# First attention of a two-block transformer: the sum of a modulation row moved behind a head pair's projection products

## The chip, the cores and the metric

The kernel runs on one core of a Trainium2 chip. The time is device microseconds of one execution, from start to end. Three runs of the kernel before took 1410.66, 1416.59 and 1410.87 us; the median is 1410.87 us. One execution was profiled.

## The reference, cut to what matters

The reference is two transformer blocks over 256 tokens of width 1024, batch 1, in float32. The first block is modulated: a vector `c` goes through a matrix `w_ada` of 1024 x 6144, and the six pieces of the result shift, scale and gate the two halves of the block. Its mixer has two attentions of eight heads each; the first is ordinary softmax attention here (there is one block of 256 keys), with a bias by distance.

```python
c_act = jax.nn.silu(c)
mod = c_act @ w_ada[l] + b_ada[l]
sh_m, sc_m, gt_m, sh_f, sc_f, gt_f = jnp.split(mod, 6, axis=-1)
h = modulate(rms_norm(x, g_mix[l]), sh_m, sc_m)
proj = jnp.einsum('bsd,de->bse', h, w_in[l])
qa, ka, va, qb, kb, vb, gate_logits = jnp.split(proj, splits, axis=-1)
oa = moba_attention(...)            # first attention: qa, ka, va
ob = stick_breaking_attention(...)  # second attention: qb, kb, vb
...
x = x + gt_m[:, None, :] * mixed
```

## The kernel before, in words

Every large product is done in three parts: a float32 matrix is split into a high part and a remainder, and high times high, high times remainder and remainder times high are added up in PSUM (L2808 to L2812). A unit is 4 x 128 rows by 512 columns of a weight matrix. SyncE's queue loads it into one of three `raw` buffers, ScalarE writes its high part (`split_hi`, L2077), VectorE its remainder (`split_lo`, L2339), and TensorE then runs 24 matmuls on it: 4 row tiles, 2 tiles of 128 tokens, 3 parts. In the stretch in question three split buffers go round, and a step that works on unit u first orders the splitting of unit u + 2 (`split_ahead`, L249).

The order of the work is written out by hand. `build_plan` adds steps to one list, and each engine goes through that list and issues its own share of each step. A step that stands earlier in the list stands earlier in every engine's queue; an engine works through its queue in order, and stands still at an instruction whose semaphores have not come.

The first attention is `softmax_heads` (L446 to L497). It works on pairs of heads. For a pair it issues the products of queries and keys (`qk`), which VectorE turns into logits (L2581); then a filler; then the transposes of the probabilities of the pair before (`probturn`, L2979, three 128x128 transposes for each head, read out by ScalarE at L2207); then the exponentials of the new pair (ScalarE, L2202); then another filler; and then the products of the older pair with its values (`pv`). The transposes of even heads go to PSUM bank 2, those of odd heads to bank 3. Before it writes a bank, TensorE waits until the bank's last tenant has been read (`wait_free`, L1788).

The fillers (the list `fa`, L1224) put other work between the attention's steps: the projection of `qb`, `kb` and `vb`, each in two units of 24 matmuls into banks 6 and 7, whose results ScalarE copies out (L2179); and the modulation rows 4 to 9, which are needed only later. For such a row VectorE multiplies `w_ada` by the column `c_act` and adds up over eight tiles in `ada_acc` (L2448, L2450). A `quarter` (L1180) is half of that, four tiles; POOL loads the next half from HBM in two pieces, as soon as VectorE is through with the piece that it replaces (L1952). After two quarters `sum_next` (L1173) issues the sum over the 128 partitions (`adasum`): TensorE waits for `ada_acc`, multiplies it by a matrix of ones into bank 3 (L2890), and VectorE adds the result to `gate_rows` (L2468). For rows 4 and 5 that is one 128x512 float32 product.

The fillers in turn: `qb` first unit with the first quarter of row 4; `qb` second unit with the second quarter of row 4; and then the step of the change, with the sum of row 4, the first quarter of row 5 and the first unit of `kb`. This third filler stands between the `qk` products of heads 2 and 3 and the transposes of the probabilities of heads 0 and 1.

Of the kernel before, what the change touches and what calls it, by code (L numbers as in the profile page):

```python
# [266 lines left out]
def build_plan(W):  # L267
# [937 lines left out]
    def chunk_fillers(name, i, dst, mode):  # L1205

        made = {}

        def first():
            made["uses"], made["parts"] = w_in_chunk(i, dst, mode, (6, 7))  # L1210
            r[name] = made["uses"]
            add_proj(made["parts"][0])

        def second():
            add_proj(made["parts"][1])
        return first, second

    heads_of = {name: chunk_fillers(name, i, i * BANK, "plain") for name, i in (("qb", 3), ("kb", 4), ("vb", 5))}
# [3 lines left out]
        turns_of("kb", 4, 12, 6, ("uses", r["kb"]))  # L1222

    fa = [[sum_next, quarter, f] for name in ("qb", "kb", "vb") for f in heads_of[name]]  # L1224
    fa += [[sum_next, turn_second], [quarter], [sum_next]]

    gates = [chunk_fillers(f"gate{i}", 6 + i, (0, BANK, 3 * BANK, 4 * BANK)[i], "tanh") for i in range(4)]
# [399 lines left out]
def program(nc, consts, x, c, w_ada, b_ada, g_mix, w_in, w_br_moba, w_br_sb, w_out, rel_bias, g_ffn, w_up,  # L1627
            w_conv, b_conv, w_down, g_final, norm_g, ffn_wg, ffn_wu, ffn_wd, even_w_in, even_w_out,
            even_lambda, even_subln, odd_w_in, odd_w_out, odd_rel_bias, table, out):
    with ExitStack() as ctx:  # L1630
# [7 lines left out]
        def over(name, handle_end, words, n):  # L1638
# [118 lines left out]
                                                                               "group_hidden"))  # L1757

        plan = build_plan(dict(w_ada=w_ada[0], w_in=w_in[0], w_br_moba=w_br_moba[0], w_br_sb=w_br_sb[0], w_out=w_out[0],
                               w_up=w_up[0], w_down=w_down[0], ffn_wg=ffn_wg, ffn_wu=ffn_wu, ffn_wd=ffn_wd,  # L1760
                               even_w_in=even_w_in, even_w_out=even_w_out, odd_w_in=odd_w_in, odd_w_out=odd_w_out))
# [1363 lines left out]
```

How the kernel before makes its waits and increments, by code:

```python
        def wait_ready(eng, use):  # L1776
            if use.unit is not None:
                eng.wait_ge(unit_used, use.unit + 1)
            else:
                eng.wait_ge(psum_ready[use.bank], use.ready)
# [1 line left out]
        def wait_read(eng, use):  # L1783
            name, value = use.read_by
            eng.wait_ge(psum_read[use.bank] if name == "psum_read" else named[name], value)
# [6 lines left out]
        def wait_past(eng, free):  # L1793
            for f in free:
                if isinstance(f, int):
                    eng.wait_ge(unit_used, f + 1)
                else:
                    wait_ready(eng, f)
# [1 line left out]
        def wait_rows(eng, what):  # L1801
            if what in raw_slot:
                eng.wait_ge(weight_loaded[raw_slot[what]], landed[what])
                return raw[:, raw_slot[what], :]
            e = plan.early.index(what[1])
            eng.wait_ge(early_landed[e % FIRST], 16 * (e // FIRST + 1))
            return early_rows[e % FIRST]
# [56 lines left out]
        @block.sync  # L1865
# [3 lines left out]
            def wait_consumed(number):  # L1869
                if isinstance(plan.ada_done[number], int):
                    sp.wait_ge(ada_used, plan.ada_done[number])
                else:
                    wait_ready(sp, plan.ada_done[number])
# [4 lines left out]
                    e = plan.early.index(what[1])  # L1878
                    if e == 2:
                        sp.wait_ge(c_act_ready, 1)
                    if e >= FIRST:
# [38 lines left out]
            def link(ins):  # L1920
                pool.wait_ge(pool_step, mark(ins))
```

## Time and profile before

| | |
|---|---|
| median of 3 runs | 1410.87 us |
| the profiled execution, whole | 1412.61 us |
| its span, first to last instruction | 1410.9 us |
| TensorE busy | 1371.5 us (97%) |
| VectorE busy | 1096.4 us (78%) |
| ScalarE busy | 817.6 us (58%) |
| mean granted TensorE clock | 0.993 of full speed |
| first attention, with fillers | about 72 to 125 us of the span |
| stretch between the `qk` products of heads 2, 3 and the next filler | 83.9 to 93.7 us |

Times in the rows count from the start of the span. A row of the timeline gives start, duration, engine, source line, operation, destination and sources, and how many equal instructions are merged in it; in brackets, how long the engine stood still before it, and on whom it waited. TensorE's rows are pipelined: the start of the next row, not the end of one, tells how fast the engine gets on.

### The profile page before, as it was taken

The page shows a single profiled execution, that of the slowest core. Times are in us where ns is not written, and L with a number is a line of the kernel's source. Part 1 is how long each engine was busy: PE and PEld are TensorE (multiplying, and loading weights), DVE is VectorE, ACT ScalarE, POOL GpSimd, SP SyncE. Part 2 cuts the span into 40 slices and gives each one's busy share as a digit, 9 for nine tenths or more (in the row PEclk, how much of TensorE's full clock was granted, in tenths as well). Part 3 has the DMA queues.
Part 4 walks back from the last instruction along what each step waited for, and adds up shares of the span by engine and source line. Part 5 has one row for each costly group of instructions (what it writes and reads, how often), then busy time and mean ns, then how long its engine had stood idle before and what let it go on. Part 6 is the DMA issues. An engine that isn't in the chain of part 4 may idle for free.

```text
span 1410.9 us, 19388 instructions
## 1 busy us (share of the span) xinstructions
PE 1371.5 (97%) x6943; PEld 1138.8 (81%) x6943; DVE 1096.4 (78%) x1565; ACT 817.6 (58%) x1301; POOL 80.3 (6%) x133
## 2 busy tenths in 40 slices
PE   4999999999999999999999999999999999999998
PEld 4878877999987888888778888888888877788886
DVE  5677787799777999669986999569996556679893
ACT  4556755755546566466576566465655567566562
POOL 3011100000000000012300000000000100000000
PEclk8999999999999999999999999999999999999999
DMA  9887556487653565745255466735747373564570
GB/s 353 287 305 257 192 174 188 147 282 248 203 185 131 183 238 166 231 131 170 99 169 169 172 222 213 234 107 203 242 151 267 116 221 120 180 204 147 201 238 30
DMA packets 160702, 274.37 MB, mean 194 GB/s; under 512 B 5953, under 2 KB 87617, under 8 KB 160609
## 3 DMA queue, kind: packets, MB, share of 16 engines
q1 hardware_dynamic: 153904, 250.86, 53.0%
q0 software_dynamic: 5552, 20.20, 4.6%
q10 hardware_dynamic: 1153, 2.07, 0.4%
q8 instruction: 57, 0.93, 0.3%
q14 instruction: 36, 0.29, 0.1%
HBM read 272.05 MB, written 1.06 MB: 194 GB/s over the span
## 4 chain that ended last, share of the span: by engine, by line
PE 68%; DVE 9%; issue 3%; DMA 2%; ACT 1%; POOL 0%; DVEq 0%; POOLq 0%; ACTq 0%; SPq 0%
PE psum L2810 17%; PE psum L2812 17%; PE psum L2811 17%; DVE w_lo L2339 3%; PE psum L2853 2%; PE psum L2852 2%; PE psum L2850 2%; PE psum L3059 2%; PE psum L3058 2%; PE psum L3057 2%; DMA raw<-in_ffn_wu_dram 1%; PE psum L3083 1%; DVE scr L2331 1%; PE psum L2907 1%; DMA raw<-in_ffn_wd_dram 1%
## 5 line engine op out<-in xcount | busy, mean ns | idle before, releaser
L2339 DVE TENSOR_TENSOR w_lo<-raw,w_hi 128x1024 fp32r<-128x1024 f32 (+2 forms) x310 | 368.0, 1232 | 72.2 <-ACT w_hi L2077 71.3
L2077 ACT ACTIVATE w_hi<-raw 128x1024 fp32r<-128x1024 f32 (+2 forms) x310 | 308.1, 1047 | 89.5 <-DMA raw<-in_ffn_wu_dram 23.7
L2810 PE MATMUL psum<-w_hi,hT_hi 128*128 128x512 f32 x712 | 287.3, 404 | 6.5 <-DVE hT_lo L2504 3.7
L2812 PE MATMUL psum<-w_hi,hT_lo 128*128 128x512 f32 x712 | 278.4, 391 | 0.0
L2811 PE MATMUL psum<-w_lo,hT_hi 128*128 128x512 f32 x712 | 278.2, 391 | 0.0
L2810 PEld LDWEIGHTS psum<-w_hi,hT_hi 128*128 128x128 f32 x712 | 134.7, 189 | 39.1 <-issue 10.0
L2812 PEld LDWEIGHTS psum<-w_hi,hT_lo 128*128 128x128 f32 x712 | 134.6, 189 | 29.1
L2811 PEld LDWEIGHTS psum<-w_lo,hT_hi 128*128 128x128 f32 x712 | 135.0, 190 | 25.7 <-issue 0.5
L2810 PE MATMUL psum<-w_hi,hc_hi 128*128 128x512 f32 x272 | 106.7, 392 | 1.6 <-DVE hc_lo L2429 1.1
L2812 PE MATMUL psum<-w_hi,hc_lo 128*128 128x512 f32 x272 | 106.0, 390 | 0.0
L2811 PE MATMUL psum<-w_lo,hc_hi 128*128 128x512 f32 x272 | 105.9, 389 | 0.0
L2339 DVE TENSOR_TENSOR lo_at<-raw,hi_at 128x1024 fp32r<-128x1024 f32 x74 | 87.3, 1220 | 8.4 <-ACT hi_at L2077 8.3
L2339 DVE TENSOR_TENSOR lo_qk<-raw,hi_qk 128x1024 fp32r<-128x1024 f32 (+1 forms) x72 | 84.0, 1208 | 5.6 <-ACT hi_qk L2077 5.6
L2077 ACT ACTIVATE hi_at<-raw 128x1024 fp32r<-128x1024 f32 x74 | 74.3, 1051 | 22.9 <-PE psum L2812 6.1
L2077 ACT ACTIVATE hi_qk<-raw 128x1024 fp32r<-128x1024 f32 (+1 forms) x72 | 71.4, 1042 | 23.7 <-DMA raw<-in_ffn_wu_dram 8.1
L2017 POOL TENSOR_TENSOR stat<-stat,minus_half 128x1 f32<-128x1 f32 (+2 forms) x24 | 17.2, 717 | 1122.5 <-DVE stat L2487 1044.5
L2235 ACT ACTIVATE PR<-psum,stat 128x256 f32<-128x256 f32 x56 | 24.2, 472 | 67.6 <-PE psum L2812 66.4
L2810 PEld LDWEIGHTS psum<-w_hi,hc_hi 128*128 128x128 f32 x272 | 51.1, 188 | 13.5 <-DVE hc_lo L2729 1.6
L2812 PEld LDWEIGHTS psum<-w_hi,hc_lo 128*128 128x128 f32 x272 | 51.1, 188 | 10.7
L2811 PEld LDWEIGHTS psum<-w_lo,hc_hi 128*128 128x128 f32 x272 | 51.1, 188 | 10.0
L2107 ACT ACTIVATE hT_hi<-psum,cols 128x128 fp32r<-128x128 f32 x96 | 27.5, 369 | 51.6 <-PE psum L2907 51.6
L2268 ACT ACTIVATE hc_hi<-psum 128x512 fp32r<-128x512 f32 (+1 forms) x32 | 17.3, 539 | 67.5 <-PE psum L3083 67.5
(301 smaller groups left out, 2864.6 us busy)
## 6 DMA issues: line engine op xcount, KB each, us to landing
raw<-in_ffn_wd_dram SPq DMA_DIRECT2D x44, 1024.0 KB, 5.0
raw<-in_ffn_wg_dram SPq DMA_DIRECT2D x56, 512.0 KB, 4.3
raw<-in_ffn_wu_dram SPq DMA_DIRECT2D x56, 512.0 KB, 5.5
raw<-in_w_up_dram SPq DMA_DIRECT2D x44, 512.0 KB, 5.0
raw<-in_w_in_dram SPq DMA_DIRECT2D x19, 1024.0 KB, 7.3
raw<-in_ffn_wg_dram SPq DMA_DIRECT2D x16, 1024.0 KB, 5.2
raw<-in_ffn_wu_dram SPq DMA_DIRECT2D x16, 1024.0 KB, 5.3
ada_raw<-in_w_ada_dram POOLq DMA_DIRECT2D x24, 512.0 KB, 5.2
```

What stands on the lines that cost most here:

```text
L2077: nc.scalar.activation(hi_of(s)[:, cs], source_of(s)[:, cs], ACT.Copy).then_inc(ready, 1)
L2107: ins = nc.scalar.activation(tiles_of(hT_hi, k0 + i, 1, a["ts"])[:, 0, :], psum[:, a["use"].bank, i * w:(i + 1) * w], ACT.Copy, scale=g)
L2339: nc.vector.tensor_tensor(lo_of(u)[:, cs], source_of(u)[:, cs], hi_of(u)[:, cs].bitcast(F32), ALU.subtract)\
L2810: nc.tensor.matmul(o, a_hi, b_hi, start=start, stop=False)
L2811: nc.tensor.matmul(o, a_hi, b_lo, start=False, stop=False)
L2812: return nc.tensor.matmul(o, a_lo, b_hi, start=False, stop=stop)
L2850: nc.tensor.matmul(o, hi[:, b], hT_hi[:, kk, :], start=kk == 0 and f % 2 == 0, stop=False, skip_group_check=True)
L2852: nc.tensor.matmul(o, hi[:, b], hT_lo[:, kk, :], start=False, stop=False, skip_group_check=True)
L2853: ins = nc.tensor.matmul(o, lo[:, b], hT_hi[:, kk, :], start=False, stop=kk == KT - 1, skip_group_check=True)
L3057: nc.tensor.matmul(o, a_hi, b_hi, start=a["start"] and k == 0, stop=False, skip_group_check=True)
L3058: nc.tensor.matmul(o, a_hi, b_lo, start=False, stop=False, skip_group_check=True)
L3059: ins = nc.tensor.matmul(o, a_lo, b_hi, start=False, stop=k == 3, skip_group_check=True)
```

## The change

In the third filler the order of the three parts is turned round: first the quarter, then the unit of `kb`, then the sum.

```diff
     fa = [[sum_next, quarter, f] for name in ("qb", "kb", "vb") for f in heads_of[name]]
+    fa[2] = [quarter, heads_of["kb"][0], sum_next]
     fa += [[sum_next, turn_second], [quarter], [sum_next]]
```

All other fillers keep their order. The new line stands ahead of the engines' code, so every later line has a number that is one higher in the changed kernel.

On TensorE, in the third filler before: the last `qk` product of head 3, then the sum of row 4 (`ada_acc,ones`), then the 24 products of the first unit of `kb`, of which the first three stand here, then the transposes of heads 0 and 1.

```order
L2961 MATMUL psum<-QK 128x256
L2890 MATMUL psum<-ada_acc,ones 128x512 [waits ones_ready,ada_halves,psum_read3]
L2810 MATMUL psum<-w_hi,hT_hi 128x512 [waits hi_half_ready,lo_half_ready,psum_read7,psum_read6]
L2811 MATMUL psum<-w_lo,hT_hi 128x512
L2812 MATMUL psum<-w_hi,hT_lo 128x512
...
L2979 MATMUL psum<-cst,attn 128x128 [waits probs_ready,psum_read2]
L2979 MATMUL psum<-cst,attn 128x128 x2
L2979 MATMUL psum<-cst,attn 128x128 [waits probs_ready,psum_read3]
```

The same place in the changed kernel.

```order
L2962 MATMUL psum<-QK 128x256
L2811 MATMUL psum<-w_hi,hT_hi 128x512 [waits hi_half_ready,lo_half_ready,psum_read7,psum_read6]
L2812 MATMUL psum<-w_lo,hT_hi 128x512
L2813 MATMUL psum<-w_hi,hT_lo 128x512
...
L2891 MATMUL psum<-ada_acc,ones 128x512 [waits ones_ready,ada_halves,psum_read3]
L2980 MATMUL psum<-cst,attn 128x128 [waits probs_ready,psum_read2]
L2980 MATMUL psum<-cst,attn 128x128 x2
L2980 MATMUL psum<-cst,attn 128x128 [waits probs_ready,psum_read3]
```

The sum has moved behind the 24 products, and the transposes of head 1, which wait for bank 3 (`psum_read3`), now stand four instructions behind the sum, which writes that bank.

On VectorE, before: the last logits of head 3, then the addition of the row's sum to `gate_rows`, then the quarter of row 5 (four instructions), then the two halves of a remainder.

```order
L2581 ISA attn,nmax<-psum,scr 128x256
L2581 ISA nmax 128x1
L2468 TENSOR_TENSOR gate_rows<-psum,gate_rows 128x512
L2448 TENSOR_SCALAR ada_acc<-ada_raw,c_act 128x512
L2450 SCALAR_TENSOR_TENSOR ada_acc<-ada_raw,c_act,ada_acc 128x512 x3
L2339 TENSOR_TENSOR w_lo<-raw,w_hi 128x1024 x2
L2450 SCALAR_TENSOR_TENSOR ada_acc<-ada_raw,c_act,ada_acc 128x512 x4
```

The same place in the changed kernel.

```order
L2582 ISA attn,nmax<-psum,scr 128x256
L2582 ISA nmax 128x1
L2449 TENSOR_SCALAR ada_acc<-ada_raw,c_act 128x512
L2451 SCALAR_TENSOR_TENSOR ada_acc<-ada_raw,c_act,ada_acc 128x512 x3
L2340 TENSOR_TENSOR w_lo<-raw,w_hi 128x1024 x2
L2469 TENSOR_TENSOR gate_rows<-psum,gate_rows 128x512
L2451 SCALAR_TENSOR_TENSOR ada_acc<-ada_raw,c_act,ada_acc 128x512 x4
```

The addition to `gate_rows`, which reads bank 3, now stands behind the quarter of row 5 and behind the remainder. The queues of ScalarE, POOL and SyncE hold the same instructions in the same order as before.

## Rows read from the trace of the kernel before

**Rows 1.** The page: busy times by engine; shares of the chain that ended last.

```profile
PE 1371.5 (97%) x6943; PEld 1138.8 (81%) x6943; DVE 1096.4 (78%) x1565; ACT 817.6 (58%) x1301; POOL 80.3 (6%) x133
...
PE 68%; DVE 9%; issue 3%; DMA 2%; ACT 1%; POOL 0%; DVEq 0%; POOLq 0%; ACTq 0%; SPq 0%
```

**Rows 2.** Windows: busy times by engine, granted clock, DMA share, GB/s.

```profile
83.90:93.10 9.20, 7.35 (x36) 5.47 (x36) 8.68 (x19) 2.98 (x4) 2.14 (x3) 1.00 0.86 302
93.10:107.90 14.80, 14.80 (x77) 11.94 (x76) 12.43 (x22) 7.49 (x16) 2.85 (x4) 1.00 0.90 304
```

**Rows 3.** Timeline of TensorE, 84 to 100 us: start, duration, instruction, idle before.

```profile
84.22 0.61 PE L2961 MATMUL psum<-QK 64*128 64x256 f32 x4
86.68 1.10 PE L2890 MATMUL psum<-ada_acc,ones 128*128 128x512 f32 x2 [1.85 <-issue]
...
87.84 0.39 PE L2811 MATMUL psum<-w_lo,hT_hi 128*128 128x512 f32 x1
...
93.42 0.49 PE L2979 MATMUL psum<-cst,attn 128*128 128x128 f32 x3
93.66 0.47 PE L2810 MATMUL psum<-w_hi,hT_hi 128*128 128x512 f32 x1
...
99.21 0.33 PE L2991 MATMUL psum<-PR,attn 128*128 128x64 f32 x2
```

**Rows 4.** Timeline of ScalarE from 84 us.

```profile
84.00 1.08 ACT L2179 ACTIVATE PR<-psum 128x512 f32<-128x512 f32 x2 [3.37 <-PE psum L2812]
84.97 2.00 ACT L2077 ACTIVATE w_hi<-raw 128x1024 fp32r<-128x1024 f32 x2
```

**Rows 5.** Timeline of VectorE, 85 to 96 us.

```profile
85.04 1.54 DVE L2450 SCALAR_TENSOR_TENSOR ada_acc<-ada_raw,c_act,ada_acc 128x512 f32<-128x512 f32 x2 [0.20 <-DMA ada_raw<-in_w_ada_dram]
...
90.00 0.69 DVE L2468 TENSOR_TENSOR gate_rows<-psum,gate_rows 128x512 f32<-128x512 f32 x1
90.72 0.49 DVE L2448 TENSOR_SCALAR ada_acc<-ada_raw,c_act 128x512 f32<-128x512 f32 x1
91.24 0.75 DVE L2450 SCALAR_TENSOR_TENSOR ada_acc<-ada_raw,c_act,ada_acc 128x512 f32<-128x512 f32 x1
...
92.11 1.54 DVE L2450 SCALAR_TENSOR_TENSOR ada_acc<-ada_raw,c_act,ada_acc 128x512 f32<-128x512 f32 x2
...
93.69 2.36 DVE L2339 TENSOR_TENSOR w_lo<-raw,w_hi 128x1024 fp32r<-128x1024 f32 x2
```

**Rows 6.** POOL's issue of the second piece of row 5; landing times of `ada_raw`.

```profile
86.87 0.71 POOL L1952 DMA_DIRECT2D ada_raw<-in_w_ada_dram  x1 [1.01 <-DVE ada_acc L2450]
...
DMA to landing us min/median/max: 4.2/5.2/7.1
```

**Rows 7.** Timeline of TensorE where its granted clock was low.

```profile
28.88 0.76 PE L2810 MATMUL psum<-w_hi,hT_hi 128*128 128x512 f32 x1 [3.51 <-DVE hT_lo L2504]
...
33.69 0.40 PE L2812 MATMUL psum<-w_hi,hT_lo 128*128 128x512 f32 x1
...
696.36 0.87 PE L2979 MATMUL psum<-cst,attn 128*128 128x128 f32 x3 [2.64 <-DVE attn L2598]
```

**Rows 8.** Windows where the granted clock (third column from the end) fell or rose.

```profile
33.50:34.00 0.50, 0.50 (x3) 0.37 (x3) 0.47 (x2) 0.00 (x0) 0.00 (x0) 0.83 1.08 406
...
47.00:47.50 0.50, 0.50 (x5) 0.35 (x5) 0.27 (x2) 0.00 (x0) 0.00 (x0) 0.82 0.64 90
...
50.50:51.00 0.50, 0.50 (x3) 0.36 (x3) 0.18 (x2) 0.50 (x2) 0.00 (x0) 0.76 0.00 0
...
695.75:696.00 0.25, 0.00 (x0) 0.00 (x0) 0.25 (x1) 0.00 (x0) 0.18 (x1) 0.71 0.00 0
...
699.25:699.50 0.25, 0.25 (x3) 0.20 (x2) 0.21 (x2) 0.25 (x1) 0.00 (x0) 0.96 0.00 0
```

**Rows 9.** Timeline: first and last of TensorE's eight waits between 94 and 246 us.

```profile
118.52 1.14 PE L2922 MATMUL psum<-cst,PR 128*128 128x128 f32 x8 [0.25 <-ACT QK L2184]
...
245.36 0.63 PE L2907 MATMUL psum<-cst,scr 128*128 128x128 f32 x4 [0.90 <-DVE scr L2495]
```

## The prediction

> **What bounds the kernel now.** First the page's busy times and the shares of its chain: TensorE is busy 97% of the span, and holds 68% of the chain that ended last [rows 1]. So what counts is when TensorE gets to its instructions; the other engines matter where it waits for them. Then the windows around the change: from 83.9 to 93.1 us TensorE is busy for 7.35 of 9.20 us, in the stretch behind it for all of 14.80 [rows 2]. The missing 1.85 us are one gap, which the timeline shows in front of the sum of row 4 [rows 3]: TensorE is through with the `qk` products at 84.83 and starts the sum at 86.68. The row puts the gap down to nothing ("issue"), but the sum needs `ada_acc`, whose last piece VectorE ends at 85.04 + 1.54 = 86.58 [rows 5], and 86.68 is 0.1 us behind that. So the sum waits for the second quarter of row 4, and the 24 `kb` products queue behind it although nothing else holds them.
>
> **What the change removes.** The products now come first. Their unit was split long before, and their banks 6 and 7 are free when ScalarE has copied `qb` out, at 84.00 + 1.08 = 85.08 [rows 4]; with the 0.1 us that a semaphore took above they start at 85.15. 24 products take 99.21 - 93.66 = 5.55 us [rows 3], to 90.70. The sum costs what it cost: from 86.68 to the second product of `kb` at 87.84 are 1.16 us, less one product (5.55 / 24 = 0.23), 0.93 us. It waits for nothing now, and ends at 91.63. The transposes of head 0 follow; before, those of head 1 and the next product stood at 93.42 and 93.66, 0.24 to 0.33 us for a head (I take 0.33). TensorE reaches the transposes of head 1 at 91.96 instead of 93.42: a lead of 1.46 us.
>
> **What it adds.** Those transposes write bank 3, where the sum now is the last tenant, and must wait until VectorE has added it to `gate_rows`. Before, that addition ran at 90.00 [rows 5], 3.4 us before the transposes, and cost nothing. Now it stands behind the quarter of row 5 and a remainder. VectorE, step by step:
> - It is through with the logits at 90.0, as before, and can begin the quarter 0.7 us sooner, since no addition is in front. That gains nothing: of the four instructions the first two ended at 91.24 + 0.75 = 91.99 and the third began at 92.11 [rows 5]. It waited for the second piece of the row, which POOL issued at 86.87 [rows 6]; 92.11 is 5.24 us later, and the median landing is 5.2. So the third begins at 92.11 again, and the quarter ends where it did, at 93.65.
> - The remainder ran from 93.69, two halves in 2.36 us [rows 5]; its high part is ready at 84.97 + 2.00 [rows 4]. The next instruction can begin about 0.08 us before that row's end, as the starts around 90 us show: 95.97.
> - The addition takes 0.69 us, to 96.66. With 0.1 us for the semaphore, the transposes of head 1 start at 96.75, against 93.42 before.
>
> So the gap of 1.85 us in front of the sum is traded for one of 96.75 - (91.63 + 0.33) = 4.8 us in front of head 1's transposes. What is queued behind them on TensorE is everything else: the second `kb` unit, the value products of heads 0 and 1, the next `qk`, the whole rest of the program. ScalarE waits with it (copies of head 1, exponentials of heads 2 and 3, the next high part). First term: 96.75 - 93.42 = **+3.3 us**. Its bounds come from the landing: at 4.2 us (the shortest of 24) VectorE would begin the quarter's second half when the first ends, and gain 0.7 us (+2.6); at 7.1 us (the longest) it would lose 1.9 us (+5.2). I take the landing of the same piece as in the trace.
>
> **The clock.** TensorE would stand still for 4.8 us. The trace has two stretches where it stood still for more than 2 us and then met work: before 28.88 us for 3.51, and before 696.36 us for 2.64 [rows 7]. In the second the granted clock left 1.00 for 0.50 (2.4 for 1.2 GHz) within 695.75 to 696.00 and was back at 699.27 [rows 8], 2.9 us after work began. In the first it had been low before, after single-column products, and was back at 33.67, 4.8 us after work began; the 11 products in between took 4.81 us [rows 7], 0.437 each instead of 0.23. A third low stretch, behind single-column products without a gap, lasted from 47.32 to 50.74 [rows 8], 3.4 us. In the gap of 1.85 us of today the clock stayed at 1.00 [rows 2]. So after 4.8 us I expect it low, and for the mean of 2.9, 3.4 and 4.8 us, 3.7 us, in which (0.437 - 0.23) / 0.437 = 0.47 of the time is lost: second term **+1.7 us**, between 0 (it doesn't fall) and 2.3 (4.8 us low).
>
> The Trainium skill (TensorE: Matmul & The Clock Gate, Part 1: The HAM clock gate) gives 426.7 ns from one 512-column matmul to the next at the low clock and 215.7 ns at the high one. By it half the time at the low clock would be lost, 1.8 us in place of 1.7 (an estimate from that page). The rows here show products that are slower at the full clock, 231 ns, so the measured ratio is kept.
>
> **Nothing else is priced.** The queues of ScalarE, POOL and SyncE are unchanged. Row 5's next loads are issued when the quarter's halves end, up to 0.3 us sooner or at the same time. VectorE's later work (row 5's second quarter, the next remainder, the logits of heads 4 and 5) begins by my working at most 2 us later than before, while TensorE is 5 us later, so none of it becomes a new wait; the sum of row 5 finds its quarter ready.
>
> **Does the delay last?** Between 94 and 246 us TensorE waits eight times, 3.7 us in all, the first and the last shown [rows 9]. Each is for a copy or a remainder that itself follows one of TensorE's own results, so it moves along. Load buffers are three deep, and are freed by work that follows TensorE too. I carry the delay to the end in full.
>
> **The sum.** +3.3 + 1.7 = +5.0 us. The profiled execution took 1412.61 us, 1410.9 of it span; it would take 1417.6. It lies 1.74 us above the median of the runs, 1410.87, so the predicted time is 1410.87 + 5.0 = 1415.9 us. That is +0.36%, less than the 0.5% (7.05 us) below which a measurement of this kernel can't tell a change from none.
>
> **Rivals.**
> - The clock stays up, or falls only as the gap ends: +3.3 us, 1414.2. For it: the fall at 695.9 came more than 2 us after TensorE had stopped, and the clock doesn't fall in every short gap. Against it: 4.8 us is longer than both gaps in the trace.
> - Part is given back: if the eight later waits [rows 9] were for work that isn't delayed, up to 3.7 us of the 5.0 are absorbed: 1412.2 at the least, some 1413 if half are. For it: VectorE is less delayed than TensorE. Against it: what they wait for (copies of transposes, remainders of fresh features) comes out of TensorE.
> - It gets faster: head 1's transposes don't wait, because VectorE reaches the addition before TensorE reaches bank 3. Then only the lead counts: 1410.87 - 1.46 = 1409.4 us. It decides at 91.96 us; the addition would have to be done by then, and stands behind two instructions that can't start before 92.11 and a remainder of 2.36. For it speaks that TensorE's gap of 1.85 us is real and is removed; against it VectorE's order.
> - The piece of row 5 lands late: at 7.1 us from its issue the first term is 5.2, with a clock that is low for 4.8 us together 5.2 + 2.3 = 7.5 us, 1418.4. For it: 86% of the DMA engines' time is taken here [rows 2]. Against it: the median of 5.2.
>
> **How the numbers follow.** The forecast 55%, the clock rival 13%, partly given back 13%, faster 6%, late landing 13%. The likeliest case alone spans 1410.87 + 2.6 + 1.3 = 1414.8 to 1410.87 + 3.9 + 2.3 = 1417.1. The range for 8 in 10 reaches to the middle of the case that gives back and to the end of the late landing: 1412.5 to 1418.4. Faster by over 0.5% would need 1403.8, which no case reaches: 1%. Slower by over 0.5% needs 1417.9: a landing and a low clock both near their ends, some two thirds of the late-landing case, 9%. Within: 90%.
>
> **What would show it right or wrong.** In the changed kernel's timeline the 24 `kb` products should start near 85.15 with a gap of 0.3 us, not 1.85, before them; the sum near 90.7; then a gap of 4 to 5 us before the transposes of head 1, which should start near 96.7, right behind the addition to `gate_rows`; and a granted clock of 0.50 for 3 to 5 us from there. The next filler's first product, at 93.66 now, should stand near 97.3, and the first value product (99.21 now) near 104. It is wrong if head 1's transposes start before 95 us, if the clock stays at 1.00, or if TensorE's lag behind the trace before is below 4 us at 246 us.

## The result: 0.33% slower, and where the profile shows it

The changed kernel takes 1416.64 us (median of 22 runs, 1414.64 to 1420.62), the kernel before 1411.88 us (22 runs, 1409.99 to 1416.59). The ratio is 1.0033, 95% interval 1.0026 to 1.0039: 4.7 us more (3.7 to 5.5). The forecast was 5.0 us more. The profiled execution of the changed kernel took 1415.25 us, 1413.5 of it span. The range given for the time, 1412.5 to 1418.4 us, holds the measured median.

Executions start the stretch at slightly different times: the last `qk` row stands at 84.22 in the trace before [rows 3] and at 83.62 here. So places are compared below by their distance from that row. The lines of the changed kernel are one higher than before.

TensorE's timeline in the changed kernel (start, duration, instruction, idle before it) answers to [rows 3].

```profile
83.62 0.61 PE L2962 MATMUL psum<-QK 64*128 64x256 f32 x4
84.59 0.47 PE L2811 MATMUL psum<-w_hi,hT_hi 128*128 128x512 f32 x1 [0.36 <-issue]
84.90 0.39 PE L2812 MATMUL psum<-w_lo,hT_hi 128*128 128x512 f32 x1
...
89.89 0.39 PE L2813 MATMUL psum<-w_hi,hT_lo 128*128 128x512 f32 x1
90.11 1.02 PE L2891 MATMUL psum<-ada_acc,ones 128*128 128x512 f32 x2
90.97 0.49 PE L2980 MATMUL psum<-cst,attn 128*128 128x128 f32 x3
96.62 0.90 PE L2980 MATMUL psum<-cst,attn 128*128 128x128 f32 x3 [5.16 <-DVE gate_rows L2469]
97.17 0.78 PE L2811 MATMUL psum<-w_hi,hT_hi 128*128 128x512 f32 x1
...
98.17 0.63 PE L2813 MATMUL psum<-w_hi,hT_lo 128*128 128x512 f32 x1
98.60 0.63 PE L2811 MATMUL psum<-w_hi,hT_hi 128*128 128x512 f32 x1
...
104.56 0.33 PE L2992 MATMUL psum<-PR,attn 128*128 128x64 f32 x2
```

The gap of 1.85 us in front of the sum has become one of 0.36, and the sum follows the products without a wait. The transposes of head 1 then wait for the addition to `gate_rows`: 5.16 us. They stand 96.62 - 83.62 = 13.00 us behind the last `qk` row; before it was 93.42 - 84.22 = 9.20. That is 3.8 us. The 24 products and what lies between them and the first value product took 5.55 us before and 104.56 - 97.17 = 7.39 now, 1.84 more; the row 98.60 follows 98.17 by 0.43 us, nearly twice the 0.227 of the products before the gap ((89.89 - 84.90) / 22).

VectorE's timeline answers to [rows 5].

```profile
83.29 3.11 DVE L2451 SCALAR_TENSOR_TENSOR ada_acc<-ada_raw,c_act,ada_acc 128x512 f32<-128x512 f32 x4 [1.76 <-DMA ada_raw<-in_w_ada_dram]
...
92.03 1.54 DVE L2451 SCALAR_TENSOR_TENSOR ada_acc<-ada_raw,c_act,ada_acc 128x512 f32<-128x512 f32 x2 [0.81 <-DMA ada_raw<-in_w_ada_dram]
93.61 2.36 DVE L2340 TENSOR_TENSOR w_lo<-raw,w_hi 128x1024 fp32r<-128x1024 f32 x2
95.88 0.68 DVE L2469 TENSOR_TENSOR gate_rows<-psum,gate_rows 128x512 f32<-128x512 f32 x1
```

The addition ends at 95.88 + 0.68 = 96.56, and head 1's transposes start 0.06 us later. In front of it stand a landing (0.81 us of waiting), the quarter's second half and a remainder.

Windows (busy time of PE, PEld, DVE, ACT and POOL, then granted clock, DMA share, GB/s) answer to [rows 8].

```profile
94.00:94.50 0.50, 0.00 (x0) 0.00 (x0) 0.50 (x1) 0.00 (x0) 0.50 (x1) 0.80 1.01 410
...
101.00:101.50 0.50, 0.50 (x3) 0.37 (x3) 0.50 (x1) 0.50 (x1) 0.36 (x1) 0.87 1.24 184
```

In the gap the clock fell from 1.00 to 0.50 (2.4 to 1.2 GHz) within 94.00 to 94.50 and rose again within 101.00 to 101.50, about 4.5 us after work began again.

The delay then stays. The last of the eight waits of [rows 9] comes 161.14 us behind the last `qk` row before, and 250.64 - 83.62 = 167.02 us now: a lag of 5.9 us: 3.8 from the hold (the wait of head 1's transposes for bank 3), 1.84 from the slow products, and the rest, within 0.1 us, from the slow transposes (97.17 - 96.62 = 0.55 us from them to the first product, 93.66 - 93.42 = 0.24 before). "Lag" means this figure in what follows, always against the one trace of before.

```profile
250.64 0.63 PE L2908 MATMUL psum<-cst,scr 128*128 128x128 f32 x4 [0.91 <-DVE scr L2496]
```

### The profile page after: what moved, and what is told of

Its sections match the earlier page's. It is cut to its first block, busy times and chain, and to the rows that moved or that the text cites. A ratio compares the mean times of both kernels' runs of the same rounds, so it can differ in the third digit from the quotient of the medians.

```text
span 1413.5 us, 19389 instructions
## 1 busy us (share of the span) xinstructions
PE 1371.2 (97%) x6943; PEld 1139.3 (81%) x6943; DVE 1097.0 (78%) x1565; ACT 816.9 (58%) x1301; POOL 80.3 (6%) x133
## 4 chain that ended last, share of the span: by engine, by line
PE 77%; DVE 4%; issue 1%; ACT 1%; POOL 0%; DVEq 0%; POOLq 0%; ACTq 0%
PE psum L2811 18%; PE psum L2813 18%; PE psum L2812 18%; PE psum L3058 4%; PE psum L3060 4%; PE psum L3059 4%; PE psum L2854 2%; PE psum L2853 2%; PE psum L2851 2%; PE psum L3084 1%; DVE w_lo L2340 1%; PE psum L2908 1%; PE psum L2980 1%; PE psum L3067 1%; PE psum L3009 0%
```

## The experiments

The theory: the products gain their 1.5 us, but head 1's transposes must wait for bank 3, whose reader stands late on VectorE; the gap costs its own length and lowers the clock. Rivals: VectorE's new order costs by itself; the clock has no part in it; the delay is given back later.

**Another bank for the sum.** `sum_low` is the kernel's own form of `sum_next` that writes bank 4.

```diff
-    fa[2] = [quarter, heads_of["kb"][0], sum_next]
+    fa[2] = [quarter, heads_of["kb"][0], sum_low]
```

> The changed kernel with one word more: the sum of row 4 goes to PSUM bank 4 instead of bank 3; order of all queues as in the changed kernel. Theory (the transposes of head 1 are held by bank 3 until VectorE, two jobs later, has added the sum to gate_rows, and the clock falls in that gap): no gap of 5 us, the transposes of head 1 follow head 0's at once, the clock stays at 1.00, and only the lead is left: 1.5 us faster than before, ratio 0.999. Rival (the cost lies in the later place of the products, of the sum or of the addition itself, whatever the bank): a gap of about 5 us stays somewhere ahead of the second kb unit and the ratio stays near 1.0033.

Measured: 1414.39 us (12 runs) against 1413.2; ratio 0.9999 (0.9988 to 1.001; the quotient of the two medians is 1.0008, inside the interval). The profiled execution, 1416.47 us, is the slowest of the twelve. TensorE's timeline:

```profile
84.45 0.61 PE L2962 MATMUL psum<-QK 64*128 64x256 f32 x4
...
91.81 0.82 PE L2980 MATMUL psum<-cst,attn 128*128 128x128 f32 x6
103.14 2.04 PE L2891 MATMUL psum<-ada_acc,ones 128*128 128x512 f32 x2 [2.89 <-issue]
```

The transposes of both heads run in one go, 7.4 us behind the `qk` row: with another bank the hold is gone, though the addition comes even later than in the changed kernel (97.97 - 84.45 = 13.52 us behind `qk` against 95.88 - 83.62 = 12.26). So the bank is the cause. But the gain I expected, a ratio of 0.999, isn't shown: it lies at the edge of the interval. In this execution row 5's sum waits 2.89 us, where it had found its quarters ready before. VectorE shows why:

```profile
92.81 0.48 DVE L2449 TENSOR_SCALAR ada_acc<-ada_raw,c_act 128x512 f32<-128x512 f32 x1 [1.62 <-DMA ada_raw<-in_w_ada_dram]
...
97.97 0.68 DVE L2469 TENSOR_TENSOR gate_rows<-psum,gate_rows 128x512 f32<-128x512 f32 x1
...
101.50 1.54 DVE L2451 SCALAR_TENSOR_TENSOR ada_acc<-ada_raw,c_act,ada_acc 128x512 f32<-128x512 f32 x2 [0.82 <-DMA ada_raw<-in_w_ada_dram]
```

The quarters go at the pace of their landings, so a TensorE that is earlier waits at the next sum. How long is partly chance: the piece at 92.81 came 7.1 us after its issue at 85.72. In the trace before the same quarter ended 97.71 + 3.12 - 84.22 = 16.61 us behind `qk`. TensorE was ready for the sum at 103.14 - 2.89 - 84.45 = 15.80; with the landings of before it would have waited about 0.9 us (an estimate from the two traces). In that gap the clock fell, and stayed low for 6 us after it (windows):

```profile
102.00:102.50 0.50, 0.00 (x0) 0.00 (x0) 0.47 (x2) 0.00 (x0) 0.00 (x0) 0.76 0.85 332
...
109.00:109.50 0.50, 0.50 (x4) 0.41 (x3) 0.47 (x1) 0.00 (x0) 0.47 (x1) 0.91 1.05 393
```

**The gap filled with work.** Twenty useless 512-column products stand between the transposes of head 0 and head 1.

```diff
+            if bias == "moba" and h == 1:
+                pl.add("fill", use=r["va"][0], times=20)
             pl.add("probturn", n=n0 + h, k=k, use=use, diff=diff, scaled=None)
...
+                elif kind == "fill":
+                    wait_read(pe, a["use"])
+                    for _ in range(a["times"]):
+                        nc.tensor.matmul(psum[:, a["use"].bank, :], hT_hi[:, 0, 0:P],
+                                         hT_hi[:, 0:2, :].rearrange("p a n -> p (a n)"), start=True, stop=True)
```

> The changed kernel with 20 matmuls of 512 columns that nobody needs (about 4.6 us) between the transposes of head 0 and those of head 1, into bank 0, which is free there. Theory (a hold of 3.8 us and 2.1 us from the low clock): the transposes of head 1 start at the same place behind the addition to gate_rows, near 96.6 us, the clock stays at 1.00, and the run is 2.1 us shorter than the changed kernel: ratio 1.0018. Rival (the clock costs nothing, the whole delay is the hold): ratio 1.0033 as in the changed kernel.

Measured: 1415.31 us (12 runs), ratio 1.0013 (1.0003 to 1.0023). TensorE's timeline and one window:

```profile
83.86 0.61 PE L2969 MATMUL psum<-QK 64*128 64x256 f32 x4
...
91.47 4.81 PE L2878 MATMUL psum<-hT_hi 128*128 128x512 f32 x20
96.94 0.55 PE L2987 MATMUL psum<-cst,attn 128*128 128x128 f32 x3 [0.66 <-DVE gate_rows L2471]
...
248.92 0.63 PE L2915 MATMUL psum<-cst,scr 128*128 128x128 f32 x4 [0.94 <-DVE scr L2498]
```

```profile
95.00:100.00 5.00, 4.34 (x21) 3.35 (x20) 3.39 (x5) 2.48 (x10) 0.00 (x0) 1.00 0.88 326
```

Head 1's transposes come as late as in the changed kernel (13.08 against 13.00 us behind `qk`), the clock stays at 1.00, and the lag at the last wait is 248.92 - 83.86 - 161.14 = 3.9 us instead of 5.9. So the clock's share is 2.0 us here, and the ratios agree with it: they differ by 0.0020 of the time, 2.8 us, with wide intervals. More work on TensorE made the changed kernel faster.

**The same filling in the kernel before.** There nothing is held, so the twenty products should simply cost their time. The branch for `fill` is the one above.

```diff
+            if bias == "moba" and h == 1:
+                pl.add("fill", use=r["va"][0], times=20)
...
```

> The kernel before (sum in front) with the same 20 matmuls that nobody needs, at the same place: a pure delay of about 4.6 us on TensorE, with no gap and no fall of the clock. Theory (TensorE's queue carries a delay here to the end in full): 4.6 us slower than before, ratio 1.0033, and a lag of 4.6 us at the transposes that stand at 245.4 us in the trace before. Rival (later waits give part of it back): ratio 1.0007 to 1.0020.

Measured: 1417.23 us (12 runs), ratio 1.0023 (1.0012 to 1.0034), 3.3 us (1.7 to 4.8). TensorE's timeline:

```profile
85.07 0.61 PE L2968 MATMUL psum<-QK 64*128 64x256 f32 x4
87.80 1.10 PE L2897 MATMUL psum<-ada_acc,ones 128*128 128x512 f32 x2 [2.12 <-issue]
...
94.45 4.82 PE L2877 MATMUL psum<-hT_hi 128*128 128x512 f32 x20
99.10 0.49 PE L2986 MATMUL psum<-cst,attn 128*128 128x128 f32 x3
...
251.02 0.63 PE L2914 MATMUL psum<-cst,scr 128*128 128x128 f32 x4 [0.92 <-DVE scr L2497]
```

From the first filling product to the transposes are 4.65 us. Those transposes lag by 99.10 - 85.07 - 9.20 = 4.83 us, for the filling and a gap that was 0.27 us longer, and the last wait of [rows 9] by 251.02 - 85.07 - 161.14 = 4.81. Up to there a delay of this place is carried in full, and the eight waits absorb none of it. To the end of the program this run doesn't decide: its ratio lies between the 1.0033 of the theory and the 1.0020 of the rival, and the interval holds both.

**Only the addition late.** The sum stays in front of the products on TensorE; only VectorE has the new order. The step is cut in two, one for each engine; the helper `sum_here`, which issues one engine's share, is left out here.

```diff
-    fa[2] = [quarter, heads_of["kb"][0], sum_next]
+    fa[2] = [sum_here("pe"), quarter, heads_of["kb"][0], sum_here("dve")]
```

> Half of the change: on TensorE the sum stays in front of the kb products as before; on VectorE the addition to gate_rows stands behind the quarter and the remainder as in the changed kernel. Theory (VectorE's order makes the cost): the gap of 1.85 us in front of the sum is back, the transposes of head 1 are held until near 96.7 us again, a gap of about 3 us, with a shorter fall of the clock: 3.3 to 5 us slower than before, ratio 1.0024 to 1.0036. Rival (TensorE's order makes the cost): as before, ratio 1.000.

Measured: 1417.82 us (12 runs), ratio 1.0026 (1.0016 to 1.0037). TensorE's timeline:

```profile
83.70 0.61 PE L2974 MATMUL psum<-QK 64*128 64x256 f32 x4
86.88 1.40 PE L2903 MATMUL psum<-ada_acc,ones 128*128 128x512 f32 x2 [2.57 <-issue]
...
97.35 0.55 PE L2992 MATMUL psum<-cst,attn 128*128 128x128 f32 x3 [1.96 <-DVE gate_rows L2481]
```

Head 1's transposes stand 13.65 us behind `qk`, later than with both parts. TensorE's order doesn't matter for them; the place of bank 3's reader on VectorE sets the time. In this execution the clock fell behind the gap of 2.57 us, so the second gap is shorter, but its end is still the addition's.

**Only the sum late.** The other half: the products first, and VectorE's addition in its old place, in front of row 5's quarter.

```diff
-    fa[2] = [quarter, heads_of["kb"][0], sum_next]
+    fa[2] = [sum_here("dve"), quarter, heads_of["kb"][0], sum_here("pe")]
```

> The other half of the change: on TensorE the sum stands behind the kb products as in the changed kernel; on VectorE the addition to gate_rows stands in front of the quarter and the remainder as before. Theory (VectorE's order makes the cost): VectorE waits for the sum until about 91.7 us, the transposes of head 1 start near 92.5 instead of 93.4, a lead of 0.9 us, and the clock stays up; but row 5's quarters come 1.7 us later on VectorE, so that the sum of row 5 may wait up to 2 us: 0.9 us faster to 1.1 us slower than before, ratio 0.9994 to 1.0008. Rival (the sum's place on TensorE makes the cost): ratio near 1.0033.

Measured: 1415.15 us (1411.14 to 1419.09, 12 runs) against 1412.83; ratio 1.0017 (1.0008 to 1.0027). TensorE's timeline, then VectorE's:

```profile
84.03 0.61 PE L2974 MATMUL psum<-QK 64*128 64x256 f32 x4
...
92.34 0.55 PE L2992 MATMUL psum<-cst,attn 128*128 128x128 f32 x3 [0.46 <-DVE gate_rows L2481]
...
102.41 1.10 PE L2903 MATMUL psum<-ada_acc,ones 128*128 128x512 f32 x2 [1.90 <-issue]
```

```profile
91.59 0.69 DVE L2481 TENSOR_TENSOR gate_rows<-psum,gate_rows 128x512 f32<-128x512 f32 x1 [1.70 <-PE psum L2903]
```

The hold of 5 us is gone. Now VectorE waits 1.70 us for the sum, and the quarter behind it is late; row 5's sum waits 1.90 us where it had not waited. The profiled execution (1411.14) is the fastest of the twelve, with a lag of 1.1 us. The measured ratio is above my expectation (0.9994 to 1.0008), and the trace of that execution can't show why the others were slower. A clock that falls in the gap of row 5's sum, as in the kernel with the other bank, would do it; that is not shown.

**The changed kernel once more.**

> The changed kernel once more, beside the half above on the same chip: ratio 1.0026 to 1.0039 as measured, the gap before the transposes of head 1 about 5 us, and the clock at 0.50 for 3 to 5 us behind it.

Measured: 1418.08 us (5 runs), ratio 1.0033 (1.0021 to 1.0045). TensorE's timeline, then VectorE's:

```profile
84.50 0.61 PE L2962 MATMUL psum<-QK 64*128 64x256 f32 x4
...
98.45 0.90 PE L2980 MATMUL psum<-cst,attn 128*128 128x128 f32 x3 [6.11 <-DVE gate_rows L2469]
```

```profile
92.55 0.49 DVE L2449 TENSOR_SCALAR ada_acc<-ada_raw,c_act 128x512 f32<-128x512 f32 x1 [2.08 <-DMA ada_raw<-in_w_ada_dram]
```

Here it was the first piece of row 5 that landed late: POOL issued it at 85.56, 7.0 us earlier. The quarter ended 93.08 + 2.32 - 84.50 = 10.90 us behind `qk`, 0.95 later than in the first execution (92.03 + 1.54 - 83.62 = 9.95), and the transposes stand 0.95 us later too. The hold grew to 13.95 - 9.20 = 4.75 us, the lag to 6.6. So the rival of the late landing is part of the range from run to run, and here all of the late landing ended up in TensorE's gap.

**Sums of rows 4, 5 and 6 behind the products.** If the lead is lost at row 5's sum, that sum should go behind its products too, and row 6's likewise.

```diff
+    fa[2] = [quarter, heads_of["kb"][0], sum_low]
+    fa[4] = [quarter, heads_of["vb"][0], sum_low]
-    fa += [[sum_next, turn_second], [quarter], [sum_next]]
+    fa += [[turn_second, sum_low], [quarter], [sum_next]]
```

> From the findings so far: the sum of row 4 in bank 4 and behind the products, as in the run with the other bank; the sum of row 5 moved in the same way behind the first unit of vb (bank 4 too); and the sum of row 6 behind the transposes of qb and kb. Theory (the lead of 1.5 us was lost at the sum of row 5 because that row's loads are paced by their landing and not by TensorE, and the gap there let the clock fall): with those sums behind work that is ready there is no gap over 0.5 us up to the end of the first attention, the clock stays at 1.00, and at the transposes that stand at 245.4 us in the trace before TensorE is 0.7 to 1.9 us ahead (part may go at the sum of row 7, whose margin before was 0.7 us): ratio 0.9987 to 0.9995. Rival (the lead is lost to something else): a gap of 2 to 3 us turns up elsewhere before 125 us, and the ratio is 1.000 or above.

Measured: 1417.06 us (8 runs) against 1413.3; ratio 1.0026 (1.0014 to 1.0038). TensorE's timeline, VectorE's, and a window in the gap:

```profile
105.36 1.02 PE L2892 MATMUL psum<-ada_acc,ones 128*128 128x512 f32 x2
...
119.78 1.87 PE L2895 MATMUL psum<-ones,ada_acc 128*128 128x1 f32 x8 [2.71 <-DVE nmax L2583]
```

```profile
113.67 3.11 DVE L2452 SCALAR_TENSOR_TENSOR ada_acc<-ada_raw,c_act,ada_acc 128x512 f32<-128x512 f32 x4 [1.58 <-DMA ada_raw<-in_w_ada_dram]
116.82 2.36 DVE L2341 TENSOR_TENSOR w_lo<-raw,w_hi 128x1024 fp32r<-128x1024 f32 x2
```

```profile
119.00:119.50 0.50, 0.00 (x0) 0.00 (x0) 0.50 (x4) 0.00 (x0) 0.00 (x0) 0.50 0.90 139
```

Row 5's sum no longer waits. The lead lasts to 116 us, and then the same trap closes once more: bank 4, into which row 6's sum goes, still holds `qk` products of head 6, which VectorE turns into logits only behind a quarter and a remainder. Gap 2.71 us, clock low, lag 6.4.

**Row 6's sum later.** It stands one filler further down, behind value products. The edit is against the run above.

```diff
-    fa += [[turn_second, sum_low], [quarter], [sum_next]]
+    fa += [[turn_second], [quarter], [sum_low]]
```

> Changed order in which the sums of rows 4, 5 and 6 stand behind the products of heads kb0, vb0 and the value products of the next pair, and row 4's sum is written into the bank that nothing queued reads. Theory (a hold comes only where the sum's bank is still read by work queued behind it, and a gap in front of a sum costs its length and, if the clock falls, as much again): no gap over 0.5 us on TensorE between 84 and 118 us, the lead of about 1.5 us over the kernel before is kept until the logits of heads 6 and 7, which stand on VectorE behind the second quarter of row 6 and end at about 119; so 0.5 to 1.5 us stay. Time against before 0.9985 to 0.9998. Rival (VectorE's chain of landings sets the pace, so any lead on TensorE becomes a gap of 2 to 3 us at a later wait, where the clock falls): a gap over 2 us between 100 and 122 us with the clock at 0.50 behind it, and 1.000 to 1.003.

Measured: 1413.96 us (11 runs) against 1413.55; ratio 1.0002 (0.9992 to 1.0011). TensorE's timeline and two windows:

```profile
83.48 0.61 PE L2963 MATMUL psum<-QK 64*128 64x256 f32 x4
...
106.71 1.12 PE L2892 MATMUL psum<-ada_acc,ones 128*128 128x512 f32 x2 [1.74 <-DVE nmax L2583]
...
119.58 0.43 PE L2993 MATMUL psum<-PR,attn 128*128 128x64 f32 x2 [0.41 <-ACT attn L2209]
...
121.03 1.05 PE L2895 MATMUL psum<-ones,ada_acc 128*128 128x1 f32 x8
```

```profile
124.50:125.00 0.50, 0.50 (x5) 0.38 (x4) 0.50 (x1) 0.00 (x0) 0.13 (x1) 0.79 1.00 369
...
131.50:132.00 0.50, 0.50 (x3) 0.36 (x3) 0.47 (x2) 0.49 (x3) 0.22 (x1) 0.88 0.00 0
```

No version came out clearly faster than the kernel before. Row 5's sum waits 1.74 us, because bank 4 holds `qk` products whose logits stand behind a late quarter on VectorE; the clock stays up there. In the run above the same order had no such wait: there the quarter landed in time. At 119.58, 119.58 - 83.48 = 36.10 us behind `qk` against 120.73 - 84.22 = 36.51 for the same products before, a lead of 0.4 us is left. Then the clock falls (window 124.50 to 125.00) where no wait in front of it is longer than 0.41 us, behind the eight single-column products of row 6's sum and a few short waits, and rises only near 131.5. Whether those products are the cause isn't shown: the trace before has the same eight at 116.28, and its clock stays at 1.00 behind them. The lag at the last wait is 4.2 us in this execution, which is the median one of the eleven, and yet that median is close to the one of before. My rival had a gap and a fall behind it; the fall came without its gap.

## Why the prediction was right

- **The time.** Forecast 1415.9 us, measured 1416.64. The median of before rose by 1.0 us, from 1410.87 in three runs to 1411.88 in 22. With so many runs the interval is clear of 1, so the 0.5% that the prediction took for the least that can be told was too coarse. That 4.7 us came so near to 5.0 is in part luck: up to 246 us the terms are 0.9 us larger than forecast, and 1.2 us of them don't show in the medians.
- **The products first.** Forecast from 85.15 with a gap of 0.3 us, the sum at 90.7. In the time of the trace before (0.60 added) they start at 85.19 behind 0.36 us, the sum stands at 90.71.
- **Head 1's hold, the first term.** Forecast +3.3, with bounds of 2.6 and 5.2 from the landing; measured +3.8 here and +4.75 in the second execution. The mechanism is the forecast one, to the instruction: the kernel with another bank takes it away, and the one with only the addition late makes it whole. The 0.5 us come from before the landing: row 4's quarter ended 83.29 + 3.11 - 83.62 = 2.78 us behind `qk`, against 86.58 - 84.22 = 2.36 before, so the piece that the last half waits for was asked for 0.4 us later. The change doesn't touch that quarter, so this is chance.
- **The clock, the second term.** Forecast 0.50 for 3 to 5 us, 3.7 taken, +1.7 us; measured 4.5 us of work at 0.50, 1.84 us on the products and 0.3 on the transposes; with the gap filled 2.0 less. So the two later marks came late: in the time of the trace before, the next filler's first product stands at 97.77 instead of 97.3, the first value product at 105.16 instead of near 104. The rival in which the clock stays up is out. The ground for the fall was thin, though: the prediction counted two stretches of more than 2 us, and the same trace has three more at its start (waits of 3.23, 7.67 and 4.07 us before the rows at 3.23, 11.14 and 16.41), where the granted clock is given as 1.00. (The sixteen products behind the last of them stand 0.22 us apart and the next eight 0.11, so the clock there isn't certain.) The prediction set the measured ratio of two product times against figures of the Trainium skill (TensorE: Matmul & The Clock Gate, Part 1: The HAM clock gate), 426.7 ns from one to the next at the low clock and 215.7 at the high one. These traces agree on the first (0.43 us) and not on the second (0.227), and the measurement decides.
- **Nothing else priced.** Row 5's sum found its quarters ready in the changed kernel, as forecast: the delay itself saw to that. Where the delay was removed, that sum became the next wait, which I had not written down as the limit of the gain.
- **The lead.** In the rival that gets faster I valued it at the full 1.46 us. That was wrong, and the forecast didn't depend on it. The trace before had it to read: row 5's second quarter ended at 97.71 + 3.12 = 100.83 and its sum began at 101.45, so a lead of more than about 0.5 us would have waited there. No kernel here kept the lead in its median, since VectorE's chain of quarters, paced by landings, meets TensorE again at row 5's sum or at a bank that waits for logits.
- **Carried in full.** To 246 us this is shown, by the eight waits that kept their size and by the filling in the kernel before. Behind it the lag shrinks in all nine profiles, by 0.1 to 2.7 us up to the end of the span; in the profiled pair it is (1413.5 - 83.62) - (1410.9 - 84.22) = 3.2 us there. A good part of that is the trace before, which waits at 530.00 for VectorE. VectorE had stood still for the landing of a block of weights and works without a gap from there (its row, then TensorE's):

```profile
524.62 2.36 DVE L2331 TENSOR_TENSOR scr<-raw 128x1024 f32<-128x1024 f32 x2 [1.95 <-DMA raw<-in_ffn_wu_dram]
...
530.00 0.47 PE L2810 MATMUL psum<-w_hi,hc_hi 128*128 128x512 f32 x1 [1.07 <-DVE hc_lo L2429]
```

At this product the nine others wait 0.34 us at most, and their lag falls by 0.7 to 1.2 us, by as much in the kernel with only the sum late (a lag of 0.9 just before it) as in the second execution of the changed kernel (6.5). A delay given back would look otherwise. The rest, between 1.5 us less lag and 0.8 us more, stays open. So does the end of the account: the local lag was 5.9 and 6.6 us, the medians differ by 4.7, and one trace of before can't tell whether its first 246 us are typical. The two profiled executions don't settle it either: that of before lies 0.73 us above its median, that of the changed kernel 1.39 below.

## What to carry to other kernels

Before a step is moved behind the work that waits for it, look at what it writes: if the next thing queued needs that buffer, the place of the buffer's *reader* on the other engine sets the price, not the place of the step. Removing a wait pays only as far as the next thing that the same chain feeds; here that chain went at the pace of landings, and the 1.5 us won in front came back as 1.9 and 2.9 us of waiting a stage later in the two traces that show it, late landings among them. And price an idle gap on TensorE twice, once for its length and, if the clock falls in it, once for the slow products behind it: here filling the gap with useless products was faster than leaving it.

## What the runs showed that I had not expected

- The clock's fall isn't told by the length of a gap alone. It stayed at 1.00 with gaps of 1.85 (before), 1.74 (row 5's sum in the last kernel) and 2.12 us (the filled kernel before), fell with gaps of 2.57, 2.71 and 2.89 us, and fell once near 124.8 us with no wait over 0.41 us in front of it. One gap stands in all ten traces, before the transposes at 696.36 in the trace before [rows 7], 2.61 to 2.68 us long. The clock fell there in nine of them, and stayed at 1.00 in the first execution of the changed kernel:

```profile
699.90 0.52 PE L2980 MATMUL psum<-cst,attn 128*128 128x128 f32 x3 [2.68 <-DVE attn L2599]
```

- That fall cost nothing: from these transposes to the next ones that wait are 709.72 - 696.36 = 13.36 us in the trace before and 713.26 - 699.90 = 13.36 where the clock stayed up. There TensorE waited for VectorE instead, 1.26 us at 704.97 against 0.21 at 701.43 before.
- The landing that sets row 5's quarter differs between executions of the same kernel: the first piece had landed by 89.94, when VectorE was free for it, in the first profiled execution of the changed kernel, and 7.0 us behind its issue, at 92.55, in the second.
- A kernel can lose less by doing more: 4.81 us of useless products brought the changed kernel from a ratio of 1.0033 to 1.0013.
